# Two-block transformer kernel: the second block's projection in another order, with taps split by engine, a diagonal of root values in the norms, and identity products ahead of the norms' splits

## The reference

```python
hl = modulate(rms_norm_2(x_lat, norm1_g), sh1, sc1)            # norm, then scale and shift
pa, q, k, v, pc = project(hl)                                   # one product with w_in, q and k normed by head, rotated
o  = diff_attn(q, k_all, v_all, lam)                            # two softmaxes, second one times lam, subtracted
ya = chunk_gmlp(pa)                                             # gelu, layer norm, a 128x128 token product as gate
yb = rms_norm_2(o, subln_g) * (1 - lam_init)
yc = silu(layer_norm(dwconv(a * sigmoid(g), conv_w)))           # 31 taps over the tokens, 256 channels
x  = x + g1 * (concat(ya, yb, yc) @ w_out)
h2 = modulate(rms_norm_2(x, norm2_g), sh2, sc2)
x  = x + g2 * ((silu(dwconv(h2 @ w_gate)) * (h2 @ w_val)) @ w_down)
```

## Time and profile before

| | before |
|---|---|
| median of 3 runs | 2413.66 us (2406.47 to 2415.41) |
| profiled execution, its own time | 2416.61 us |
| its span | 2415.0 us |
| PE busy | 2214.7 us (92%) |
| PE weight loads, beside it | 1797.3 us (74%) |
| DVE busy | 1416.3 us (59%) |
| ACT busy | 1051.4 us (44%) |
| POOL busy | 306.3 us (13%) |
| granted clock, mean of the span | 0.951 |
| DMA | 349.28 MB, mean 145 GB/s |

### The profile page before, as it was taken

The page is one execution under the profiler, slowest core; times in us unless marked ns, Lnnn a source line. Parts: engine busy times, 40 slices in busy tenths (PEclk is TensorE's granted clock), DMA queues, the critical chain, the costliest instruction groups (busy, mean ns, idle before and its releaser), DMA issues. The chain is left out here.

```text
span 2415.0 us, 31203 instructions
## 1 busy us (share of the span) xinstructions
PE 2214.7 (92%) x11948; PEld 1797.3 (74%) x11948; DVE 1416.3 (59%) x2231; ACT 1051.4 (44%) x1745; POOL 306.3 (13%) x313
## 2 busy tenths in 40 slices
PE   8999899899999999898998987779999998778998
PEld 6777677678777777676887765568888886658987
DVE  4655485544456554854554698654655338766764
ACT  4445544444445455554444454522332225454442
POOL 0005421000000054220000171000000002400000
PEclk9999899999999989999999998789999999889999
DMA  7645334465656543344655321222332334234554
GB/s 234 203 165 163 118 122 141 147 214 191 221 191 208 167 166 123 131 144 172 220 181 179 112 69 53 71 63 98 104 129 88 121 98 148 61 115 140 192 175 148
DMA packets 171842, 349.28 MB, mean 145 GB/s; under 512 B 11824, under 2 KB 23216, under 8 KB 171696
## 3 DMA queue, kind: packets, MB, share of 16 engines
q1 hardware_dynamic: 171696, 347.29, 43.9%
HBM read 346.19 MB, written 1.05 MB: 144 GB/s over the span
## 5 line engine op out<-in xcount | busy, mean ns | idle before, releaser
L825 DVE TENSOR_TENSOR wlo<-wraw,whi 128x1024 fp32r<-128x1024 f32 (+1 forms) x535 | 646.0, 1220 | 704.4 <-ACT whi L1022 702.0
L1022 ACT ACTIVATE whi<-wraw 128x1024 fp32r<-128x1024 f32 (+1 forms) x552 | 557.8, 1027 | 600.1 <-PE psum L1779 279.2
L1779 PE MATMUL psum<-whi,act_h 128*128 128x512 f32 (+2 forms) x1424 | 576.2, 405 | 20.1 <-DVE wlo L825 8.2
L1779 PE MATMUL psum<-wlo,act_h 128*128 128x512 f32 (+2 forms) x1424 | 556.0, 390 | 0.0
L1779 PE MATMUL psum<-whi,act_l 128*128 128x512 f32 (+2 forms) x1424 | 555.2, 390 | 0.0
L1779 PEld LDWEIGHTS psum<-whi,act_h 128*128 128x128 f32 x1424 | 274.2, 193 | 88.3 <-issue 22.5
L1779 PEld LDWEIGHTS psum<-whi,act_l 128*128 128x128 f32 x1424 | 273.1, 192 | 57.3
L1779 PEld LDWEIGHTS psum<-wlo,act_h 128*128 128x128 f32 x1424 | 274.2, 193 | 48.9
L1779 PE MATMUL psum<-act_h,whi 128*128 128x512 f32 (+1 forms) x704 | 243.8, 346 | 15.3 <-DVE cacc L1400 6.3
L1779 PE MATMUL psum<-act_l,whi 128*128 128x512 f32 (+1 forms) x704 | 239.7, 340 | 0.0
L1779 PE MATMUL psum<-act_h,wlo 128*128 128x512 f32 (+1 forms) x704 | 239.0, 340 | 0.0
(11 more groups left out here) (268 smaller groups left out, 2759.0 us busy)
## 6 DMA issues: line engine op xcount, KB each, us to landing
wraw<-in_w_in SPq DMA_DIRECT2D x136, 512.0 KB, 4.3
wraw<-in_w_gate SPq DMA_DIRECT2D x104, 512.0 KB, 4.1
wraw<-in_w_mod_pieces SPq DMA_DIRECT2D x96, 512.0 KB, 4.8
wraw<-in_w_ffn_in SPq DMA_DIRECT2D x80, 512.0 KB, 4.5
wraw<-in_w_ffn_out SPq DMA_DIRECT2D x44, 512.0 KB, 4.5
wraw<-in_w_down SPq DMA_DIRECT2D x44, 512.0 KB, 4.3
wraw<-in_w_val SPq DMA_DIRECT2D x40, 512.0 KB, 4.3
wraw<-in_w_branch SPq DMA_DIRECT2D x32, 512.0 KB, 4.8
```

Source lines behind the costliest of these rows:

```text
L825: eng.tensor_tensor(wlo[:, i, 0:st.n, 0:st.w], wraw[:, st.s % RING_W, 0:st.n, 0:st.w], whi[:, i, 0:st.n, 0:st.w].bitcast(F32), ALU.subtrac ...
L1022: nc.scalar.activation(whi[:, d % RING_S, 0:st.n, 0:st.w], wraw[:, s % RING_W, 0:st.n, 0:st.w], ACT.Copy).then_inc(sem("slab_rounded"), 1)
L1779: return nc.tensor.matmul(out, lhsT, rhs, start=start, stop=stop)
```

## The change

1. A new step `warm`, with n products of the identity with itself, 128x128 in plain fp32, into bank 7, which nobody reads. 14 of them stand before the splits of norms 2, 3 and 4 of the first block; 40 before those of the first norm of the second block, 24 before those of its other three. PE waits for nothing but the bank.
2. `norm2` makes on DVE, per tile, `diag` = identity x root (128x128) instead of `p` = x x root (128x1024). `modsplit` on PE is a plain fp32 product of x's block (stationary) with `diag`, which is the transposed block times the root, instead of a transpose of `p`.
3. Of the eight `modsplit`, five stand before slab 0, two before slab 1, one before slab 2 (`between`), in all norms of the second block. The `ysplit` steps likewise, and the w_out product takes its slabs in the order 0, 6, 2, 4 of k.
4. The projection's products are in the order gq, gc, gk, ga, gv. `cglu` and `cT` stand at 8 and 9. The taps are two kinds of steps: `c_taps`, DVE's half, in groups of four at 9, 10, 11, 12, 16, 17, 18, 19; and `c_taps_slow`, ACT's and POOL's half, in groups of three at 10 to 20. q's sums and scales stand at 4, 5, 6, 7, 7, k's at 12, 13, 14, 15, 15, `qkT2` and `gelu` at 16.
5. In the attention, `subln` and its two parts stand at the end of the iteration, `agate` behind the stream's i = 2 instead of first, `cback` at 4 instead of 3, the silu at 6 instead of 5.
6. After the norm before the FFN the product's banks start anew at 0.

```diff
+def warm(pl, n):
+    return Step(kind="warm", n=n, waits=[("psum_free7", pl.uses[7])])
...
-def gemm(pl, weight, layer, act, tiles, nk, col0, width, evac, row0=0, kt0=0, ready=(), turned=False, **more):
+def gemm(pl, weight, layer, act, tiles, nk, col0, width, evac, row0=0, kt0=0, ready=(), turned=False, order=None, **more):
...
-        for k in range(0, nk, SLAB_K):
+        for at, k in enumerate(order):
...
+            if n > 1:
+                pl.steps.append(warm(pl, 14))
...
+            pl.steps.append(warm(pl, 40 if l == i == 0 else 24))
...
-            pl.steps += ss
-            return {st.k: [("mod_lo", st.lo)] for st in ss}
-
-        ready = norm(0, 4, l > 0)
+            return {st.k: [("mod_lo", st.lo)] for st in ss}, between(ss)
+
+        def between(ss):
+            return [(0, st) for st in ss[:5]] + [(1, st) for st in ss[5:7]] + [(2, st) for st in ss[7:]]
+
+        ready, ss = norm(0, 4, l > 0)
...
-        gc = project(C_C, T, ready)
-        gq = project(C_Q, T)
+        gq = project(C_Q, T, ready)
+        gc = project(C_C, T)
...
-        parts = [Step(kind="c_taps", l=l, tiles=T, banks=ct.banks, n=taps[i:i + 4], last=i + 4 >= C_CONV)
-                 for i in range(0, C_CONV, 4)]
+        wide = [Step(kind="c_taps", l=l, tiles=T, banks=ct.banks, n=taps[i:i + 4], last=i + 4 >= C_CONV)
+                for i in range(0, C_CONV, 4)]
+        slow = [Step(kind="c_taps_slow", l=l, tiles=T, banks=ct.banks, n=taps[i:i + 3]) for i in range(0, C_CONV, 3)]
...
-        for i, (g, tiles, at) in enumerate(((gq, T, 8), (gk, 4, 13))):
+        for i, (g, tiles, at) in enumerate(((gq, T, 4), (gk, 4, 12))):
...
-            qk += [(at + 1 + t, Step(kind="qk_scale", t=t, **more)) for t in range(tiles)]
+            qk += [(at + 1 + min(t, 2), Step(kind="qk_scale", t=t, **more)) for t in range(tiles)]
...
-        others = [(5, cglu), (6, ct)] + [(at, st) for at, st in zip((7, 7, 11, 12, 12, 17, 17, 18), parts)]
-        others += qk + [(17, gelu), (18, qkt), (18, aln[0]), (19, aln[1])]
+        others = ss + [(8, cglu), (9, ct)] + list(zip((9, 10, 11, 12, 16, 17, 18, 19), wide))
+        others += [(10 + n, st) for n, st in enumerate(slow)]
+        others += qk + [(16, qkt), (16, gelu), (18, aln[0]), (19, aln[1])]
         others.sort(key=lambda v: v[0])
-        pl.steps += weave(gc + gq + gk + ga + gv, others)
+        pl.steps += weave(gq + gc + gk + ga + gv, others)
...
+            behind = []
...
-                    att += pending[:1]
+                    behind += pending[:1]
...
-                        att.append(subs[-1])
+                        behind.append(subs[-1])
...
+            att += behind
...
-        residual("w_out_2", "act2", KD, 0, {st.k: drained(st.bank) for st in ss}, True)
-
-
-        ready = norm(1, T, True)
+        residual("w_out_2", "act2", KD, 0, {st.k: drained(st.bank) for st in ss}, True, between(ss), order[::SLAB_K])
+
+
+        ready, ss = norm(1, T, True)
...
-        pl.turns = tuple(range(7))
+        pl.turns, pl.gemm_banks = tuple(range(7)), 0
...
-                        dve.tensor_scalar(p[:, t, 0:D], x[:, t, :], rstd4[:, t:t + 1], None, ALU.mult
+                        dve.tensor_scalar(diag[:, t, :], ident[:, :], rstd4[:, t:t + 1], None, ALU.mult
...
+                if st.kind == "warm":
+
+                    need(pe, st.waits)
+                    for i in range(st.n):
+                        dot(psum[:, 7, 0:P], ident[:, :], ident[:, :])
...
+                if st.kind == "modsplit":
+
                     need(pe, st.waits)
                     fill(pe, st.bank)
-                    a = st.k * P if st.kind == "modsplit" else st.col
                     for t in range(st.tiles):
-                        ins = turn(psum[:, st.bank[0], t * P:(t + 1) * P], p[:, t, a:a + P])
+                        ins = dot(psum[:, st.bank[0], t * P:(t + 1) * P], x[:, t, st.k * P:(st.k + 1) * P], diag[:, t, :])
+                    ins.then_inc(full(st.bank), 1)
```

More of the change, by code:

```diff
@@ L179, in gemm @@
             banks.append(pl.gemm_bank())
-        for k in range(0, nk, SLAB_K):
+        for at, k in enumerate(order):
             n = min(SLAB_K, nk - k)
-            last = k + n == nk
+            last = at == len(order) - 1
             st = Step(kind="slab", s=len(pl.slabs), weight=weight, layer=layer, row=row0 + k, n=n, col=col0 + a, w=w,
-                      act=act, kt=kt0 + k, tiles=tiles, banks=banks, first=k == 0, last=last, c=c, a=a, evac=evac,
+                      act=act, kt=kt0 + k, tiles=tiles, banks=banks, first=at == 0, last=last, c=c, a=a, evac=evac,
                       turned=turned, **more)
@@ L531, in plan_second @@
                 stream += mod_ride(pl, pl.gemm_turn())
-            if i == 3:
+            if i == 2:
+                agate = Step(kind="agate", l=l, tiles=T, n=aln[0].n, banks=[pl.gemm_bank(), pl.gemm_bank()])
+                stream.append(agate)
+            if i == 4:
                 cback = Step(kind="cback", l=l, tiles=T, banks=[pl.gemm_bank() for i in range(T // 2)])
```

33 lines of the change are left out of this document (18 added, 15 removed).

## The result

The changed kernel took 2390.53 us in the median of 4 runs (2388.90 to 2394.88) against 2413.59 us: 23 us less, ratio 0.9915, 95% interval 0.9895 to 0.9935. Its profiled execution has a span of 2389.3 us against 2415.0. Run again later beside other kernels it took 2395.24 us against 2412.00 there, ratio 0.9924 (0.9909 to 0.9939). By the ratios the change is worth 18 to 20 us, by the medians 17 to 23; the forecast was 32, with a range that holds both times.

The account below looks back on a forecast made before the run. It took PE, 92% busy, as the bound, with each wait costing idle time and a low clock behind it. Terms from -9 to 0 summed to -32 us: 2382 us, 8-in-10 range 2364 to 2402.

Parts of the forecast that it names:

- rival D: Half of the gains goes at PE's next wait, since DVE owes a `wlo` to every slab: 2397 us, chance 0.18.
- Warm products: Identity products at 0.25 us fit into PE's norm waits and keep its clock up: -3 us over three first-block norms.
- Diagonal: At the second block's norms, 0.3 us a tile on DVE instead of 0.69, so splits may start 1.5 us earlier.
- Norm before FFN, layer 0: Slab 0 starts earlier through free banks, five splits ahead, earlier splits and full clock: -9 us, between -4 and -11.
- Layer 1's -1.6: Norm before the FFN in layer 1, with two tiles: earlier splits and better clock, less woven splits, -1.6 us.
- First norm: Second block's first norm: 3 us earlier by splits and clock, less 3.0 for the weave: 0, kept at +2 to -4.
- Projection, layer 0, -7.5: Last k scale 24 us earlier by fewer taps ahead, attention four slabs behind slab 16: -7.5 us, from -16 to +11.
- Rival A: The k scale isn't earlier, as reordering only moves DVE's backlog, and two more slabs follow each wait: 2413 us, chance 0.10.
- Projection, layer 1, -2: k scale's wait ends 14 us earlier, with transposes and four slabs behind it: -2 us, from -6 to +12.
- Attention, -5 and -2.5: New attention order wins a third of 17 us PE idle in layer 0, half of that in layer 1.
- Woven y splits, -1.5: 12 of 16 y split transposes come behind the first slab's start at full clock: -1.5 us for both layers.
- Rival B: Identity products cost 0.5 us each at the low clock and overrun the norm waits: 2428 us, slower, chance 0.04.

Follow-up runs that it names:

- a_old_att: The changed kernel with the attention's order of before (subln, root and scale ahead, agate first, cback and silu one earlier): 2397.11 us, ratio 0.9935.
- c1: The changed kernel with the gmlp layer norm's scaling moved from ahead of the attention's first scores to right ahead of the gate: 2391.74 us, ratio 0.9915.
- c3: The changed kernel with gmlp scaling at the gate, layer 1's old projection order, and DVE's last three layer 0 taps behind the gate: 2388.55 us, ratio 0.9919.
- a_noweave: The changed kernel with all eight splits of norms and y again ahead of the first slab, banks still anew at the FFN: 2387.66 us, ratio 0.9912.

## Why the prediction was right

The direction and the bounds were right, and so was the largest single term. The sum was 9 to 15 us too large: the terms for the order of the projection and of the attention were too large, and in layer 1 the order of the projection even went the other way. Some 5 us in the first block, where 3 were forecast, made up for a little of it. The second measurement, 2395.24, lies nearer to rival D's 2397 than to the forecast's 2382, and the first one between the two.

- **Warm products.** Their price, 0.25 us, was right (0.23). "They fit" was right: 0.55 us of wait is left at 456.83. The gain in the first block, 3, was too small: some 5 us, with -6.0 in the mean of twelve profiles and -1.2 in the mean of the two without. It was forecast as 1.0 at each of three norms; it came as some 5 at norm 2, where a second wait went with the first, and at most about 1 at each of the other two. In the second block they give 4.9.
- **Diagonal.** A tile takes 0.28 us, forecast 0.3; four take 0.87, since they overlap, and that is 1.9 us earlier, forecast 1.5 to 2.
- **Norm before FFN, layer 0.** Forecast -9, measured -9.1 and -9.0, but the step that put three woven splits among what brings it was empty. Taken out one at a time, the banks are worth 8.0, the diagonal 2.0, the warm products 1.5, and the weave nothing; they overlap, since these add up to more than 9. Without the weave and with banks 0 to 3, PE goes through all eight splits at DVE's pace and straight into slab 0. Layer 1's -1.6 was -2.1.
- **First norm.** Forecast 0. Slab 0 starts 3.9 us earlier by its own (1338.39 to 1323.43 is 15.0, of which 11.1 come from the first block), and 3 go into the woven splits: within the bounds.
- **Projection, layer 0, -7.5.** The mechanism was seen right up to its end: the wait ends 101.6 us behind slab 0, forecast 100.6; the transposes take 9.6, forecast 11; the attention begins 7.8 us earlier than before, counted from slab 0 (1456.5 and 1479.22). The step that failed is the one that books this as the kernel's gain, "four slabs later, 1471.8, the attention and gate follow". It stops there, because PE finds DVE with eight taps of 11.54 us and four scalings of 5.50 still ahead of the scores, and waits 5.19. What the order is worth is 3.2. Rival A had the reason (a backlog moved, not removed) and the wrong place for it (the k scale's own wait, which ends 26 us earlier than in the old order); rival D had the place, the next wait, with taps and scalings where it named a `wlo`.
- **Projection, layer 1, -2.** Here the step that failed is the size of the k scale's gain: 14 us earlier were forecast, 10.8 came against the old order, and the two slabs more and the longer transposes behind it cost 13.9, forecast 12. The order loses 3.7 us in place of gaining 2. The forecast's price of a tap of half width, 0.6, stands in no row; its records take 0.47 us.
- **Attention, -5 and -2.5.** 2.2 in each layer (a_old_att), in place of a third and a sixth of the idle time. The forecast took PE's idle time for what an order can win. That DVE's queue and the chain from scores to mix set it instead is argued from c1 and c3, not shown by itself.
- **Woven y splits, -1.5.** No run takes them out alone; a_noweave takes them out together with the other woven splits and is no slower.
- **The page's rules.** The transpose mode four times faster for fp32 (Trainium skill, "TensorE: Matmul & The Clock Gate", Terms): here a plain product is 0.23 us and a transpose 0.11 at full clock, twice. The lock of the shared port (Trainium skill, "SBUF — State Buffer", Who interferes with whom): the records agree that DVE's two-input instructions take about twice as long or more beside POOL's adds, though not that it is a lock. Leaving out the adds, with ACT's weights for them, is worth 24 us in layer 0 and 9 in layer 1, more than every edit of this change to those stages; the forecast put it at 14 at most, as a delay of the k scale alone.
- **Its sums.** 1 us before 2196.32 is 2195.3, not 2195.1; the low end of the projection, -16, comes to -17 by its own terms; a third of 17 is 5.7, taken as 5. Half of the distances to the low ends is 17 us, so the forecast's own range of 2370 is narrower than it says. None of this changes the account.

Rival B, slower by identity products at the low clock, fell with the first window: 1.00.

## What to carry to other kernels

Before an order is changed to shorten a wait, add up the busy time of the engine that is waited for over the whole stretch until something else binds: here 172 of 217 us before and 173 of 217 after, so mostly the place of the wait moved. What shortened this stretch was taking time off that engine's instructions, or moving a piece of its queue to a place where it held nobody up; another piece, put at a worse place, lost twice its own length. A short wait of PE can be worth more than its length, as at norm 2, and need not be, as at norms 3 and 4: cover it with plain products, and measure each. Let a product behind a group of splits start in banks that the splits don't use.

## What the runs showed of the hardware

- Two engines' instructions beside each other: single records of DVE's tap of 128x502 take 0.74 us alone and up to 1.76 beside POOL's adds; four scalings of 128x256 take 1.67 us alone and 5.50 beside them; and the earlier trace rows showed the same for one multiplication, 0.69 and 1.74.
- TensorE stays at full clock through 48 records of identity products (1.00 in their 5.8 us), and through 32 transposes that follow full-clock slabs (3.65 us in a_few_slow, 1.00). Behind the wait of 16.47 us the same 32 took 5.11, with the clock at 0.50 in the first 2 us and 0.85 in the 3.2 behind them.
- The first block of one and the same program took 4.4 us more in one execution than in another, and over twelve programs with the same first block its end spread over 9 us. The scatter lies mostly in two stretches, up to 431 us and from 739 to 1087 us, while the stage of norm 2 repeats within 0.5 us. Which waits in those two stretches decide it was not tried.
